# Router logits from scaled, not yet normalized x; one root per token; GpSimd makes the normalized rows

## What is computed

```python
x = x + gt1 * mix                                  # mix = merged @ w_out
h = rms_norm(x, g_ffn) * (1.0 + sc2) + sh2          # sh2, sc2: per sequence, from c @ w_ada
p_grp = softmax(h @ w_rg + b_rg)                    # 4 groups: the best is taken
e_logits = h @ w_re + b_re                          # 32 experts: the best 2 of the group
x = x + gt2 * routed_experts(h, expert_ids, combine)
```

## Time and profile before

| | us |
|---|---|
| median of 3 runs | 1198.66 |
| lowest and highest | 1194.31, 1199.92 |
| profiled execution, its own time | 1199.18 |
| its span | 1197.5 |
| TensorE busy | 1012.2 (85%) |
| VectorE busy | 419.6 (35%) |
| ScalarE busy | 421.9 (35%) |
| GpSimd busy | 113.7 (9%) |

### The profile page before, as it was taken

One profiled execution on the slowest core, in us unless ns is written; L12 is line 12 of the kernel. 1 busy time (PEld: TensorE's weight loads), 2 busy tenths in 40 slices (PEclk: granted clock), 3 DMA queues, 4 the chain that ended last, 5 costly groups with the idle time before them and its releaser, 6 DMA issues.

```text
span 1197.5 us, 21552 instructions
## 1 busy us (share of the span) xinstructions
PE 1012.2 (85%) x7426; PEld 618.3 (52%) x7427; DVE 419.6 (35%) x1119; ACT 421.9 (35%) x715; POOL 113.7 (9%) x209
## 2 busy tenths in 40 slices
PE   4899999899979977777779999999986997777775
PEld 1667677377554333323357767747755533333333
DVE  1136632222441433333343483231235143232334
ACT  2111554300314554445431135531022454444443
POOL 1321003000100000000023110210010000000000
PEclk9799998989978999889988999998996999898998
DMA  9973224973622999999994223398320199999991
GB/s 383 391 271 106 106 106 153 390 288 111 247 99 116 422 422 422 422 421 422 422 394 149 106 106 106 108 359 363 141 71 1 41 422 421 423 421 422 422 407 41
DMA packets 47482, 318.73 MB, mean 266 GB/s; under 512 B 6050, under 2 KB 7394, under 8 KB 10306
## 3 DMA queue, kind: packets, MB, share of 16 engines
q1 hardware_dynamic: 41904, 304.57, 63.2%
q0 software_dynamic: 3712, 10.89, 2.7%
q10 hardware_dynamic: 1810, 2.51, 0.6%
HBM read 315.44 MB, written 2.51 MB: 265 GB/s over the span
## 4 chain that ended last, share of the span: by engine, by line
PE 54%; DMA 26%; DVE 6%; issue 6%; ACT 4%; PEld 1%; POOLq 1%; DVEq 0%; SPq 0%; POOL 0%; PEldq 0%; ACTq 0%
DMA ring<-wstream 26%; PE ps L529 18%; PE ps L590 7%; PE ps L910 5%; PE ps L862 4%; PE ps L562 3%; PE ps L896 2%; PE ps L663 2%; PE ps L765 2%; ACT work L1053 1%; PE ps L597 1%; PE ps L885 1%; PE ps L815 1%; ACT work L985 1%; PEld ps L885 1%
## 5 line engine op out<-in xcount | busy, mean ns | idle before, releaser
L910 PE MATMUL ps<-ring,work 128*32 128x512 f32 x1024 | 149.4, 693 | 95.6 <-DMA ring<-wstream 90.5
L529 PE MATMUL ps<-h,ring 128*128 128x288 f32 x512 | 134.0, 416 | 0.7 <-ACT work L995 0.7
L529 PE MATMUL ps<-work,ring 128*128 128x288 f32 x512 | 129.4, 416 | 3.8 <-DVE work L1303 2.9
L910 PEld LDWEIGHTS ps<-ring,work 128*32 128x32 f32 x1024 | 30.0, 117 | 174.6 <-issue 174.5
L590 PE MATMUL ps<-h,ring 128*128 128x288 f32 x416 | 110.3, 423 | 10.7 <-ACT h L1009 6.3
L529 PEld LDWEIGHTS ps<-work,ring 128*128 128x128 f32 x512 | 99.7, 195 | 32.8 <-issue 4.8
L985 ACT ACTIVATE work<-ps 128x288 f32<-128x288 f32 (+5 forms) x124 | 54.8, 459 | 164.6 <-PE ps L590 77.0
L529 PEld LDWEIGHTS ps<-h,ring 128*128 128x128 f32 x512 | 96.8, 194 | 29.5 <-issue 3.8
L1455 DVE COPY yb<-ps 128x256 f32<-128x256 f32 x64 | 27.2, 425 | 229.5 <-PE ps L896 229.5
L1107 ACT ACT_TABLE_LOAD x64 | 82.1, 1283 | 56.2 <-issue 56.2
L590 PEld LDWEIGHTS ps<-h,ring 128*128 128x128 f32 x416 | 82.8, 200 | 35.6 <-issue 9.1
(11 more groups left out here) (226 smaller groups left out, 1084.1 us busy)
## 6 DMA issues: line engine op xcount, KB each, us to landing
ring<-wstream SPq DMA_DIRECT2D x288, 1024.0 KB, 18.1
work<-pages POOLq DMA_DIRECT2D x32, 192.0 KB, 8.6
work<-pages POOLq DMA_DIRECT2D x32, 128.0 KB, 2.7
cs<-consts SPq DMA_DIRECT2D x1, 1218.0 KB, 8.6
x<-x_in SPq DMA_DIRECT2D x1, 1152.0 KB, 5.4
out_y<-h ACTq DMA_DIRECT2D x2, 576.0 KB, 2.8
out_vp<-v ACTq DMA_DIRECT2D x2, 256.0 KB, 5.7
sm<-small POOLq DMA_DIRECT2D x2, 194.0 KB, 7.0
```

The source lines that it names most:

```text
L529: last = mm(out, w[:, (k0 + k) * stride:(k0 + k) * stride + 128], rhs(k), start=(k == 0), stop=(k == n - 1))
L910: last = mm(pgu[32 * c:32 * c + 32, :], xs[:, k, :], ring[:, slots[k // 4], c * 512:(c + 1) * 512], start=(k < 4), stop=(k >= 4), skip_gro ...
```

## The change

Five things are changed, in each layer. (a) VectorE also scales the 256 prompt columns of each x tile by the gain into h during the output stage; TensorE multiplies these h tiles, not yet normalized, with the router's weights, three small matmuls per tile (`route_logits`), one tile behind the output job; tokens are on the partitions at once, and the jobs "router" and "logits" with their copies go. (b) sh2 @ W is made ahead of the projections by eight matmuls and spread to the tokens by three more; VectorE adds the router's bias to it. (c) The squares are summed to one column per block of 96 tokens; mean, root and reciprocal work on 96 x 3, and VectorE multiplies the logits by the reciprocal and adds the shift. Three matmuls spread the reciprocal back over the partitions, and ScalarE copies it into `rms`. (d) GpSimd, which had nothing to do here, multiplies h by `rms` (and adds the shift of the samples), and ScalarE adds the shift of the prompt; this runs beside the choice of the experts. (e) "rank" comes ahead of the six turns of h; job "next" goes into the bank `pzs` and is cut in two, 6 pieces ahead of the rank and 2 behind the turns; the gather runs half by half (all k of the first 288 slots, then of the second), and `sel` is made in the same halves, so that the first gathers wait for the first half alone (R_SEL0).

```diff
+GATHERS = [(k, hf) for hf in range(2) for k in range(KD)]
+TURNS = (0, 2, 4, 1, 3, 5)
+NEXT_EARLY = 6
...
+                logits.wait(g, l)
+                rms_kept.wait(g, l)
+                step(scaled, nc.gpsimd.tensor_tensor(h[:, :, NP:T], h[:, :, NP:T], bc(rms[:, NP:T].unsqueeze(1), [128, KD, NS]), ALU.mult))
+                hs = by_seq(h[:, :, NP:T], KD)
+                step(scaled, nc.gpsimd.tensor_tensor(hs, hs, bc(mod[:, SH2:SH2 + KD, 1:NCOND].unsqueeze(3), [128, KD, NB, TS]), ALU.add))
+                for k in range(KD):
+                    scaled.up(nc.gpsimd.tensor_tensor(h[:, k, 0:NP], h[:, k, 0:NP], rms[:, 0:NP], ALU.mult))
...
+                banks.wait_drained(pe, l, "mt1")
+                for k in range(KD):
+                    last = mm(py[0:NCOND, 112:148], mod[:, SH2 + k, :], sm[:, l, S_WR + k * 36:S_WR + (k + 1) * 36],
+                              start=(k == 0), stop=(k == KD - 1))
+                shift.up(last)
...
+                def route_logits(k):
+
+                    xgain.wait(pe, l, 2 * (k + 1))
+                    for tb in range(3):
+                        last = mm(py[0:TB, tb * 36:(tb + 1) * 36], h[:, k, tb * TB:(tb + 1) * TB],
+                                  sm[:, l, S_WR + k * 36:S_WR + (k + 1) * 36], start=(k == 0 and tb == 0), stop=(k == KD - 1),
+                                  skip_group_check=True)
...
+                    if m:
+                        route_logits(m - 1)
                 sq_added.wait(pe, l)
-                mm(pgu[:, 0:T], ones, sq_sum, start=True, stop=False)
+                for tb in range(3):
+                    mm(pgut[0:TB, tb:tb + 1], sq_sum[:, tb * TB:(tb + 1) * TB], ones[:, 0:1], start=(tb == 0), stop=False,
+                       skip_group_check=True)
...
+                ss.up(last)
+                route_logits(KD - 1)
...
+                norm2.wait(pe, l)
+                for tb in range(3):
+                    last = mm(pgu[:, tb * TB:(tb + 1) * TB], bc(dest[0:TB, 11, tb:tb + 1], [TB, 128]), ident[0:TB, 0:TB],
+                              start=True, stop=True)
+                spread_rms.up(last)
+                if l + 1 < DEPTH:
+                    next_modulation(range(NEXT_EARLY))
...
+                    xgain.up(V.tensor_scalar(h[:, m, 0:NP], x[:, m, 0:NP], gsc[:, 1, m, 0:1], None, ALU.mult))
...
-                for k in range(KD):
-                    norm2.up(V.scalar_tensor_tensor(h[:, k, 0:NP], x[:, k, 0:NP], gsc[:, 1, k, 0:1], rms[:, 0:NP], ALU.mult, ALU.mult))
...
+                r(V.tensor_tensor(lg, py[0:TB, 0:108].rearrange("p (t c) -> p t c", t=3), spread(trio(11), 36), ALU.mult))
+                shifted.wait(d, l)
+                r(V.tensor_tensor(lg, lg, lgb3, ALU.add))
...
-                banks.wait_full(d, l, "rank")
+                counted.wait(d, l)
                 ps = banks.ap(l, "rank")
-                r(V.tensor_copy(cnt[:, 0, :], ps[:, 96:128]))
+                r(V.tensor_copy(cnt[:, 0, :], pgut[:, 96:128]))
```

More of the change, by code:

```diff
@@ L112, in plan @@
     jobs += [f"out{m}" for m in range(KD)]
-    if l + 1 < DEPTH:
-        jobs += ["next"]
-    jobs += ["router", "h0", "logits"] + [f"h{n}" for n in range(1, 6)] + ["rank"]
-    for k in range(KD):
-        if k == ROWS_AT:
+    jobs += ["rank"] + [f"h{n}" for n in TURNS]
+    for i, (k, hf) in enumerate(GATHERS):
+        if i == ROWS_AT:
             jobs += ["rows"]
-        if k == NEXT_AT and l + 1 < DEPTH:
+        if i == NEXT_AT and l + 1 < DEPTH:
             jobs += ["next_t"]
-        jobs += [f"x{k}.{h}" for h in range(2)]
+        jobs += [f"x{k}.{hf}"]
     jobs += [f"bc{i}" for i in range(4)]
@@ L512, in _ @@
             for l in range(DEPTH):
-                begin(l, ss)
+                begin(l, ss, shift, logits, spread_rms, counted, next_done)
                 def weights(pair, of=l):
@@ L824, in turn_h @@
                     filled(last, f"h{n}")
-                turn_h(0)
-                ps = job("logits")
-                banks.wait_drained(pe, l, "router")
-                hold(pe, seen)
-                for tb in range(3):
-                    last = nc.tensor.transpose(ps[0:TB, tb * 36:(tb + 1) * 36], lgT[:, tb * TB:(tb + 1) * TB], ident[0:36, 0:36])
-                filled(last, "logits")
-                for n in range(1, 6):
-                    turn_h(n)
                 ps = job("rank")
@@ L839, in _ @@
                 for tb in range(3):
+                    last = mm(pgut[:, 96:128], cs[0:TB, C_ONE:C_ONE + 128], hot[0:TB, tb, :], start=(tb == 0), stop=(tb == 2))
+                counted.up(last)
+                for tb in range(3):
                     for t2 in range(tb + 1):
                         wt = C_LOW if t2 == tb else C_ONE
[L842 to L844 removed]
+                        last = mm(ps[0:TB, tb * 32:(tb + 1) * 32], cs[0:TB, wt:wt + TB], hot[0:TB, t2, :],
+                                  start=(t2 == 0), stop=(t2 == tb))
@@ L845, in _ @@
                 filled(last, "rank")
-                for k in range(KD):
-                    for hf in range(2):
-                        if k == ROWS_AT and hf == 0:
-                            ps = job("rows")
-                            route.wait(pe, l, R_WTS)
-                            for tb in range(3):
-                                last = nc.tensor.transpose(ps[0:4, tb * TB:(tb + 1) * TB], dest[0:TB, 7:11, tb], ident[0:TB, 0:TB])
-                            filled(last, "rows")
-                        if k == NEXT_AT and hf == 0 and l + 1 < DEPTH:
-                            turn_modulation("next", "next_t")
-                        ps = job(f"x{k}.{hf}")
-                        if k == 0 and hf == 0:
-                            route.wait(pe, l, R_SEL)
-                            banks.wait_drained(pe, l, "h5")
-                        for tb in range(3):
-                            last = mm(ps[:, 0:T], hrow[0:TB, tb, k * 128:(k + 1) * 128], sel[0:TB, tb, hf * T:(hf + 1) * T],
-                                      start=(tb == 0), stop=(tb == 2))
-                        filled(last, f"x{k}.{hf}")
+                for i, n in enumerate(TURNS):
+                    if i % 3 == 0:
+                        normed.wait(pe, l, normed.per[l] - KD + 4 * (i // 3 + 1))
+                    turn_h(n)
@@ new lines, in _ @@
+                if l + 1 < DEPTH:
+                    next_modulation(range(NEXT_EARLY, KD))
+                for i, (k, hf) in enumerate(GATHERS):
+                    if i == ROWS_AT:
+                        ps = job("rows")
+                        route.wait(pe, l, R_WTS)
+                        for tb in range(3):
+                            last = nc.tensor.transpose(ps[0:4, tb * TB:(tb + 1) * TB], dest[0:TB, 7:11, tb], ident[0:TB, 0:TB])
+                        filled(last, "rows")
+                    if i == NEXT_AT and l + 1 < DEPTH:
+                        turn_modulation("next", "next_t")
+                    ps = job(f"x{k}.{hf}")
+                    if k == 0:
+                        route.wait(pe, l, (R_SEL0, R_SEL)[hf])
+                        banks.wait_drained(pe, l, "h5")
+                    for tb in range(3):
+                        last = mm(ps[:, 0:T], hrow[0:TB, tb, k * 128:(k + 1) * 128], sel[0:TB, tb, hf * T:(hf + 1) * T],
+                                  start=(tb == 0), stop=(tb == 2))
+                    filled(last, f"x{k}.{hf}")
@@ L1073, in _ @@
                             a.dma_start(out, src).then_inc(rows_out, 16)
+                shift.wait(a, l, 1)
+                shift_kept.up(act(shw, py[0:NCOND, 112:148], ACT.Copy))
                 for k in range(KD):
```

152 lines of the change are left out of this document (92 added, 60 removed).

## The result

| | before | changed |
|---|---|---|
| median (runs) | 1199.29 (4) | 1185.45 (4) |
| lowest and highest | 1194.31, 1200.07 | 1184.47, 1186.1 |
| ratio of the medians, 95% interval | | 0.9891, 0.9867 to 0.9916 |
| span of the profiled execution | 1197.5 | 1183.4 |

The change makes the kernel 1.1% faster, 13.8 us; the two spans differ by 14.1. In two later comparisons the same kernel took 1186.18 us (ratio 0.9888, 0.9848 to 0.9928) and 1186.25 us (0.9905, 0.9881 to 0.9929).

A forecast was written before the change was run, and what follows sets the result against it. Weights' stream bounds the expert loop, and a chain from VectorE's read of the last output tile to the broadcasts its start; -7.8 - 11.2 + 2 x 5.0 = -9.0 us, so 1190, range 1177 to 1199 (own 1185 to 1195).

The forecast's parts named there:

- the contention: Choice of experts: each GpSimd instruction, 0.79 us, lets one two-SBUF-tensor VectorE step through; experts known at 13.5 instead of 8.8.
- TensorE's work ahead of the chain: Output stage: route calls 3.7 us, shift matmuls 0.7, spreading matmuls 0.6; together 5.0 us per layer (4.0 to 7.6).
- stage to the broadcasts: From VectorE's read of the last output tile: 47.4 and 45.8 us instead of 55.2 and 57.0; gains 7.8 and 11.2.
- Rival 4: Output stage: router calls take 1.05 us, halving the gain; +5.2, 1195; chance 0.2 together with rival 2.
- Logits and the start of the choice: Behind the last output tile's read: root and reciprocal end at 2.9, choice starts at 3.5, 10.8 us earlier.
- HOT: The chosen experts on VectorE, timed from its read of the last output tile; forecast at 13.5, bounds 8.8 and 16.4.
- rival 1: Choice: no contention to speak of, short steps slip between GpSimd's instructions; HOT at 8.8, 1178 us; chance 0.15.
- rival 2: Choice: GpSimd's instructions follow so closely that VectorE never gets in; HOT at 16.4, 1196 us; chance 0.2 with Rival 4.
- Rival 3: Choice: as rival 2, and GpSimd's operations take 1.2 us instead of 0.79; HOT at 20.5, 1204 us; chance 0.1.
- Ranks, turns, gather: Behind the choice: gather starts at 23.3 in layer 0, 22.2 in layer 1, and takes 24.0 and 23.6 us.
- TensorE comes back at the half clock: Behind TensorE's idle wait for the choice: rank matmuls at half clock, 0.175 us a record, ranks full at 17.1.
- The cover: Ahead of the turns: GpSimd's and ScalarE's work on h, last tile at about 12.8, is covered with four us to spare.

The follow-up runs named there:

- e3: Changed kernel with GpSimd's ten operations on h held until the experts are chosen; 1187.94 us.
- e8: The changed kernel itself, unedited, measured a second time; 1186.18 us, ratio 0.9888 to the kernel before.
- e12: The changed kernel itself, unedited, measured a third time; 1186.25 us, ratio 0.9905 to the kernel before.
- e4: Changed kernel with all six turns of h put ahead of the counts and ranks; 1190.52 us.
- e9: Kernel before plus ten matmuls whose result nobody reads, four between turns and ranks, six between ranks and gather; 1195.97 us, ratio 0.999 to before.
- e1: Changed kernel with GpSimd's eight prompt products of 256 columns merged into two of 1024; 1189.27 us.
- e6: Changed kernel with all eight calls of the router's matmuls behind the last output job instead of one behind each; 1186.23 us.

## Why the prediction held, point by point

The time lies 4.6 us below the forecast and inside its own range of 1185 to 1195; the mechanism was the one described, and its largest error of size, the contention, went in the change's favour in both layers. Its terms, against one profiled execution of each kernel:

| term | forecast | measured |
|---|---|---|
| TensorE's work ahead of the chain, both layers | +10.0 | +8.1 |
| stage to the broadcasts, layer 0 | -7.8 | -12.4 |
| stage to the broadcasts, layer 1 | -11.2 | -12.7 |
| expert loops (1.3 and 1.5) | 0 | +2.8 |
| sum | -9.0 | -14.1 |

**Work ahead.** I priced a route call at 0.62 by the records of the rank matmuls; the stage grew by 0.54 per call. TensorE's row for one call does say 0.62, but a row's ends overlap the next one's. In layer 0, counted from the start of the last row ahead of the shift matmuls (243.10 before, 242.73 now), t = 0 comes 4.0 later: 3.22 are the calls, 0.8 the shift matmuls (0.7 was forecast). The three spreading matmuls (0.6 of the forecast) stand behind t = 0, beside the choice, and should not have been in this term. Rival 4, calls of 1.05 us, is out.

**Logits and the start of the choice.** Forecast at t = 2.9 and 3.5, measured 2.92 and 3.5.

**The contention.** Right in kind: one held step per GpSimd instruction, reductions free. Mis-sized: HOT at 11.75 instead of 13.5. 0.6 us of it is GpSimd's pace: I took 0.79 for an instruction and put the end of all ten at 12.2; the eight products took 0.70 with the gap, 5.61 in all, and GpSimd ended at 11.6. The other 1.2 us is the count. I let three of the thirteen steps, with their reductions, run behind GpSimd's end; but one step had passed before GpSimd started, two of 32 columns (L1436) slipped through unheld, and ten were held, so that HOT, the tenth of these, came 0.1 behind GpSimd's last product. What rival 1 said of all steps, that short ones slip between, held for two of thirteen. From the 128x288 products of the earlier trace rows I had too high a price for 256 columns. The figure of the Trainium skill (GPSIMD Engine Reference, "Elementwise — side-by-side cycle accounting"), by columns an estimate of 0.56, is too low by 0.14. Rival 1, HOT at 8.8, is what e3 shows when the contention is taken away (8.53); rival 2, HOT at 16.4, does not occur: GpSimd's instructions follow each other at once, and yet a held step of VectorE ends behind each. Rival 3 needed GpSimd operations of 1.2 us; the slowest, on the 3D view, took 0.73.

**Ranks, turns, gather.** In layer 1 as forecast to 0.1 us: 8.8 from HOT to the gather (forecast 8.7), and all sixteen jobs at the full clock, 23.7 (23.6). In layer 0 the step "TensorE comes back at the half clock" failed in the profiled execution: the clock fell earlier, under the hidden pieces, so ranks and turns were at full. 7.5 from HOT to the gather instead of 9.8, which is 2.3 of layer 0's 4.6 us; the other 2.5 are HOT at 11.0 instead of 13.5 (0.7 of it because the slow spread let GpSimd start only at t = 5.15), and the gather was 0.1 longer. e8 and e12 show the forecast form in the same kernel, at 21.49; the 2.3 us were luck of this execution.

**The cover.** GpSimd's work on h was done at t = 12.3 in layer 0 and ScalarE's half a microsecond behind it, ahead of the turns at 14.0; e4 shows the wait that appears when the order takes the cover away.

**What I had not seen.** In this pair of profiles the expert loops gave 2.8 us back. In layer 0 the last weights arrive 9.1 us earlier, but the last expert block then runs at the half clock. The timeline there, changed kernel, then the kernel before in a fence of its own:

```profile
585.53 3.60 PE L973 MATMUL ps<-ring,work 128*32 128x512 f32 x16 [2.41 <-DMA ring<-wstream]
```

```profile
594.63 1.92 PE L910 MATMUL ps<-ring,work 128*32 128x512 f32 x16 [2.44 <-DMA ring<-wstream]
```

1.7 us are lost there, and the root behind the loop starts 7.4 us earlier. In layer 1 the broadcasts come 15.6 earlier and the last weights 14.1; the five zero matmuls ahead of the first expert took 2.29 against 1.47, the rest is not assigned. In e8, the same kernel, the last expert block took 1.92 and the root started at 603.74, 9.2 ahead of before's 612.92: the loss in layer 0 turns with the clock of a single block. Over both loops, e8 and e12 took 1.9 and 2.5 us less than the kernel before, not 2.8 more, so this loss is not a cost of the change.

What they lost instead lies between that root and t = 0 of layer 1, in the mixer, which takes 278.7 us in the changed kernel's first profile and 284.3 in e8 and e12 (before: 274.2, in e9 278.2). The change puts about 4 us there, its calls and shift matmuls; 5.6 more differ between executions of the same kernel. From 800 to 820 us the granted clock was 0.83 in the first profile and 0.76 in e8. One row there, changed kernel, then e8:

```profile
795.31 7.07 PE L584 MATMUL ps<-ring,sc 128*32 128x512 f32 x64 [2.03 <-DVE mod L1227]
```

```profile
796.03 8.77 PE L584 MATMUL ps<-ring,sc 128*32 128x512 f32 x64 [2.03 <-DVE mod L1227]
```

Measured with e8's profile, the sum above reads +11.0 for the first line, -9.5 and -12.8 for the two stages and -1.9 for the loops: -13.3 in all, nearly the same sum from other parts. What both profiles share is the stage behind the output: it is shorter by 22 us or more, where 19.0 was forecast.

## What to carry to other kernels

Ask of work given to GpSimd beside a chain on VectorE not how long it is but in how many instructions it comes: each of them holds back one two-tensor step of the chain for up to its own length, so cut it small (pieces of 0.42 us held the choice back by 2.1 us, pieces of 0.70 by 3.2, pieces of 2.3 by 4.6, all in layer 1, with GpSimd starting at t = 4.8, 4.5 and 5.15), and moving it behind the chain only moves the holds to the steps that stand there. Read the price of small matmuls from how much the stage grew, not from their row's length. And when a critical piece on TensorE runs at the half clock behind idle time, let hidden work or unread matmuls reach right up to it; ending three microseconds short, they bought nothing at one gather and 1.7 of 3.4 us at the other. Last, compare a small edit by the stage it changes: the same program differed by 2.9 us in one stage and by 5.6 in another from one profile to the next.

## What the runs showed of the hardware that I had not expected

VectorE and GpSimd alternate under the hold, though GpSimd's instructions stand ready one behind the other: in layer 1 of the changed kernel eight products and eight held steps of 96 columns, one behind each. Only two short steps of 32 columns slipped through. The Trainium skill (SBUF — State Buffer, "SBUF: two separate sides") says that whichever starts first has the ports for its whole instruction and the other blocks; e1's 2.10 and 2.28 us agree with that. GpSimd's pace hardly suffered: in layer 1 of e3 its products of 256 columns started 0.68 to 0.70 us apart beside held steps of 32 and of 96 columns, 0.69 where VectorE was mostly idle, and 0.75 beside VectorE's scalings of 288 columns. Even a scaling of 12 columns is held (0.71 us in layer 1 instead of 0.17 in layer 0, L1432).

The clock's fall is not tied to a place in the program. In three profiles of one kernel, with the same instructions at the same t up to the spread, the spread of layer 0 ran at the half clock once (1.59 us) and at the full one twice (0.91). Over the eleven profiles of kernels whose stage is the same up to there (the changed kernel and all its variants but e6), the slow spread came five times in layer 0 and once, in e1, in layer 1. What decides it was not found. In layer 0 it is worth 2.9 us at the gather, nearly as much as all the contention.
